# Turning the new keys and values back to token order beside the cached values instead of ahead of the cached keys

## The chip, the core and the metric

The kernel runs on one core of one Trainium2 chip. The metric is the device time of one execution in microseconds. Matrix work is on TensorE (PE), whose weight loads are shown apart as PEld; the other engines are VectorE (DVE), ScalarE (ACT), GpSimd (POOL) and SyncE (SP). Each engine runs its own instructions in the order in which they are written, and waits on semaphores. DMAs are issued by SP, ACT and POOL, and the queues of these engines are written SPq, ACTq and POOLq in the profile.

## What is computed

One inference step through two layers, for a prompt of 256 tokens and a sample group of 8 sequences with 4 new tokens each (288 columns in all). Layer 0 is a gated short convolution beside block-sparse attention; layer 1 is a Mamba-2 mixer; a SwiGLU feed-forward stands behind each. The change lies in layer 0:

```python
q, k, v = heads(q), heads(k), heads(v)       # 8 heads of 64, from h @ w_in
y_b = attend(q, k, v)
# prompt: causal attention over its own 256 tokens
# sample: the 3 best of 8 cached blocks of 256 keys, and its own new tokens
k_prompt, v_prompt = to_pages(kp), to_pages(vp)                          # outputs
k_sample, v_sample = ks.transpose(0, 2, 1, 3), vs.transpose(0, 2, 1, 3)  # outputs
```

The new keys and values are outputs of the kernel in token order. The values are also an operand of the attention. The new keys in token order are an output and nothing else; the scores read the keys as they come out of the projection.

## The kernel before

The input projection of layer 0 leaves everything with channels on the partitions and tokens on the columns, in `BIG`. Behind it stand four stages that matter here.

1. **The own rows** (PE lines 831 to 837). The 4 x 128 channels of the keys, and then of the values, are turned to token order in three tiles each: tokens 0 to 127, tokens 128 to 255, and the 32 sample tokens. That is six turns of four transposes. The results go to `KOUT` and `VTOK`, each `[128, 3, 512]`. The PSUM banks `trb[0]` and `trb[1]` are used in turn. Every turn has a number. An even number lies in `trb[0]` and is copied out by ACT (`tr_act` counts), an odd one lies in `trb[1]` and is copied out by DVE (`tr_dve` counts). `tr_open(n)` makes PE wait until the last turn in the same bank has been copied. Before the first copy ACT waits for `zeroed`, which GpSimd raises behind four memsets (lines 648 to 651); they can't start before the projection has ended, since the buffers lie over its operands. When all six are copied, GpSimd issues 20 stores of the new keys and values.

2. **The cached keys** (PE lines 957 to 971, a loop over 32 slots). A slot is 4 pages of one sequence: 16 pages, so 4 slots, for each of 8 sequences, 1 MiB per slot. PE turns the keys of a slot (line 852) and multiplies the previous slot with the queries (line 873). Two buffers hold a sequence each: `kv`, shown as Z, for the even ones and `kv2`, shown as ring, for the odd ones. The first two sequences are loaded during the projection. The keys of sequence b+2 are loaded slot by slot when PE has turned that slot of sequence b. The first turn waits until every own row is copied (line 850).

3. **The cached values** (PE lines 1013 to 1041, a loop over 8 sequences b). PE turns the probabilities of sequence b+1 (`turn_sample`, line 920), makes a step of the prompt's attention (`prompt_step`, lines 927 to 946), multiplies the values of sequence b (line 985, 32 products in `values(b)`; a last product at line 992 adds the own tokens), and turns the output of sequence b-1 (line 1001). The values use the same two buffers: the loads of sequence b+2 wait for `v_used`, slot by slot, which `values(b)` raises. SP issues 12 of the 16 loads of a sequence (line 547) and ACT issues 4 (line 1389).

   In each round b ACT does in this order: the copy of the turned probabilities (line 1447), the exponentials of the prompt step (lines 1429 and 1431), in round 1 also the exponentials of the sample scores (lines 1397 and 1403), its four loads, and the copy of the output of this round (line 1455). DVE does the masks, maxima and divisions of the prompt step, in round 1 `exp_bias` (line 1859) and the shifts of the sample scores (line 1870), and the convolution.

4. **The output projection and everything behind it.** It starts when the output of the last sequence is turned. Its weights are loaded by SP behind the last values, into the buffer that the values leave.

The order on each engine is written out by hand; there is no planner.

Of the kernel before, what the change touches and what calls it, by code (L numbers as in the profile page):

```python
# [23 lines left out]
P = 128  # L24
# [3 lines left out]
def hybrid_decoder_kernel(  # L28
# [10 lines left out]
    _, NP, D = x_prompt.shape  # L39
    NB, T, _ = x_sample.shape  # L40
    NS = NB * T
    NT = NP + NS
    KD = D // P
    NPOOL, H, PAGE, DH = cache_k.shape
# [7 lines left out]
    MQ, MK, MV = 3 * CA, 3 * CA + H * DH // P, 3 * CA + 2 * H * DH // P  # L52
# [51 lines left out]
    with ExitStack() as ctx:  # L104
# [65 lines left out]
        BIG = Area(Z).take(CC, NT)  # L170
# [7 lines left out]
        KOUT = a.take(3, H * DH)  # L178
        VTOK = a.take(3, H * DH)
# [59 lines left out]
        ident = sb("ident", [P, P])  # L239
# [45 lines left out]
        trb = [ctx.enter_context(nc.psum_tensor(f"trb{i}", [P, 512], F32)) for i in range(2)]  # L285
# [11 lines left out]
        zeroed = sem("zeroed")  # L297
# [8 lines left out]
        tr_full = sem("tr_full")  # L306
        tr_act = sem("tr_act")
        tr_dve = sem("tr_dve")
# [129 lines left out]
        TR_PAR = TR_X + KD  # L438
        TR_HIST = TR_PAR + 2
        TR_KV = TR_HIST + 4  # L440
        TR_K = TR_KV + 6
        N_K = NB * NBLK * 2

        tr_order = [("sample", 0), ("sample", 1)]
        for b in range(1, H + 1):
            tr_order += ([("sample", b + 1)] if b + 1 < NB else []) + [("prompt", b - 1)]
        TR_P = {key: TR_K + N_K + i for i, key in enumerate(tr_order)}
        TR_COA = TR_K + N_K + len(tr_order)
        TR_CO = TR_COA + 2
# [127 lines left out]
        def _(pool):  # L577
            n = [0]
# [66 lines left out]
            pool.memset(KNZ[:, :, :], 0.0)  # L645
            pool.memset(ext[:, :, 0:3], 0.0).then_inc(zeroed, 1)
            pool.wait_ge(acc_full, M_IN0)
            pool.memset(VTOK[:, :, :], 0.0)
            pool.memset(OWN_E_ROWS, 0.0)
            pool.memset(POWN[:, :], 0.0)  # L650
            pool.memset(CUP[:, :, 0:2], 0.0).then_inc(zeroed, 1)
# [6 lines left out]
                if s is stored:  # L658
                    stores[0] += 1

            pool.wait_ge(tr_act, TR_K // 2)
            pool.wait_ge(tr_dve, TR_K // 2)
            for buf, prompt, sample in ((KOUT, k_prompt, k_sample), (VTOK, v_prompt, v_sample)):
                for t in range(NP // PAGE):
                    store(prompt[0, t].rearrange("h q d -> q h d"),
# [44 lines left out]
        def _(pe):  # L710
# [12 lines left out]
            def tr_open(n):  # L723
                if n >= 2:
                    pe.wait_ge(tr_act if n % 2 == 0 else tr_dve, n // 2)
                return trb[n % 2]
# [101 lines left out]
            pe.wait_ge(consts, 3)  # L828
            project(N_IN0, M_IN0, KD, HX0, hx_ready(0), after=after_first)

            for i, m in enumerate((MK, MV)):
                for t in range(3):
                    rows = P if t < 2 else NS
                    bank = tr_open(TR_KV + 3 * i + t)
                    for c in range(H * DH // P):
                        last = pe.transpose(bank[0:rows, c * P:(c + 1) * P], BIG[:, m + c, t * P:t * P + rows], ident[:, :])
                    last.then_inc(tr_full, 1)

            def turn_keys(p):
                b, s = p // KVS, p % KVS  # L840
# [59 lines left out]
            def return_max(part):  # L900
                pe.wait_ge(d_step, part * D_STEPS + 3)
                bank, full = chain_open(part)
                pe.transpose(bank[:, 0:NH], RMT[0:NH, 2, :], ident[0:NH, 0:NH]).then_inc(full, 1)
# [113 lines left out]
            for b in range(NB):  # L1017
                if 1 <= b < NB - 1:
                    turn_sample(b + 1)
                if b and b < NB - 1:  # L1020
                    prompt_step(b)
                if b == NB - 2:
                    prompt_step(b + 1)
                if b == NB - 1:
                    prompt_step(b + 1)
                    prompt_step(b + 2)
                    turn_values(b - 1)
                    turn_history()
                values(b)
                if b == 0:  # L1030
                    turn_max(1)
                    prompt_step(0)
                if b == 1:
                    return_max(1)
                if b == 2:
                    denominators(1)
                if b == 3:
                    turn_own(1)
                if 0 < b < NB - 1:
                    turn_values(b - 1)  # L1040
# [252 lines left out]
        def _(act):  # L1293
# [40 lines left out]
            def copy_transposed(n, dst, src):  # L1334

                act.wait_ge(tr_full, n + 1)
                act.activation(dst, src, ACT.Copy).then_inc(tr_act, 1)
# [37 lines left out]
                    copy_transposed(TR_HIST + 2, hists[:, CC // 3:2 * CC // 3, :], trb[0][:, 0:n].rearrange("p (c j) -> p c j", j=3 * NB))  # L1375


            for i, (dst, t) in enumerate(((KOUT, 0), (KOUT, 1), (KOUT, 2), (VTOK, 0), (VTOK, 1), (VTOK, 2))):
                if i % 2 == 0:
                    rows = P if t < 2 else NS  # L1380
                    if i == 0:
                        act.wait_ge(zeroed, 2)
                    copy_transposed(TR_KV + i, dst[0:rows, t, :], trb[0][0:rows, :])

            def load(cache, b, s, mine):
                page = page_numbers(nc.scalar.engine, b, J4 * s + mine[0], len(mine))
# [63 lines left out]
            def copy_output(b):  # L1450
                act.wait_ge(o_full, b + 1)
                if b >= 2:
                    act.wait_ge(acc_full, marks["o", b - 2])
                act.wait_ge(d_step, b // NH * D_STEPS + 6)
                act.activation(OSB[:, b % 2, :], scb[b % 2][:, :], ACT.Copy, scale=rden[:, b:b + 1]).then_inc(o_copied, 1)
# [4 lines left out]
            for b in range(NB):  # L1460
                if 1 <= b < NB - 1:
                    copy_sample(b + 1)
                if b and b < NB - 1:
                    prompt_step(b)
                if b == NB - 2:
                    prompt_step(b + 1)
                if b == NB - 1:
                    prompt_step(b + 1)
                    prompt_step(b + 2)
                    act.wait_ge(mix_made, 1)  # L1470
                    for k in range(CA):
                        act.activation(HX1[:, k, 0, :], MIX[:, k, :], ACT.Copy).then_inc(hx_hi, 1)
                if b == 1:
                    own_exp(1)
                    for later in range(NH, NB):
                        sample_exp(later)

                for s in range(1, KVS, 2):
                    if b + 2 < NB:
                        act.wait_ge(v_used, b * KVS + s + 1)  # L1480
                        load_values(b + 2, s)
                copy_output(b)
            copy_transposed(TR_COA, coT_a[0:2 + 2 * NB, 0:2 * P], trb[0][0:2 + 2 * NB, 0:2 * P])
            split(N_OUT0)
            def post_norm(i, first_acc, kparts):
# [175 lines left out]
        def _(dve):  # L1661
# [21 lines left out]
            def copy_transposed(n, dst, src):  # L1683

                dve.wait_ge(tr_full, n + 1)
                dve.tensor_copy(dst, src).then_inc(tr_dve, 1)
# [9 lines left out]
            def rest(hx, k, col, src=None):  # L1696

                n_hx[0] += 1
                dve.wait_ge(hx_hi, n_hx[0])
                if col is None:  # L1700
                    ins = dve.tensor_tensor(hx[:, k, 1, :], src, hx[:, k, 0, :], ALU.subtract)
                else:
                    ins = dve.scalar_tensor_tensor(hx[:, k, 1, :], X[:, k, :], par[:, 0, col:col + 1], hx[:, k, 0, :],  # L1703
                                                   ALU.mult, ALU.subtract)
                ins.then_inc(hx_made, 1)
# [40 lines left out]
                last = dve.tensor_copy(KNZ[rows, :, :].rearrange("p (c r) n -> p c r n", r=2)[:, :, r, :],  # L1746
                                       BIG[rows, MK:MK + H // 2, NP:NT])
            link(last)
            for i, (dst, t) in enumerate(((KOUT, 0), (KOUT, 1), (KOUT, 2), (VTOK, 0), (VTOK, 1), (VTOK, 2))):
                if i % 2 == 1:  # L1750
                    rows = P if t < 2 else NS
                    copy_transposed(TR_KV + i, dst[0:rows, t, :], trb[1][0:rows, :])

            def move_scores(b):
                e = b % 2
# [39 lines left out]
            n = NBLK  # L1795
# [210 lines left out]
            for b in range(NB):  # L2006
                if 1 <= b < NB - 1:
                    copy_sample(b + 1)
                if b and b < NB - 1:
                    prompt_step(b)  # L2010
                if b == NB - 2:
                    prompt_step(b + 1)
                if b == NB - 1:
                    prompt_step(b + 1)
                    prompt_step(b + 2)
                    sample_output(b - 1)
                    copy_transposed(TR_COA + 1, coT_a[0:2 + 2 * NB, 2 * P:4 * P], trb[1][0:2 + 2 * NB, 0:2 * P])
                    for k in range(CA):
                        rest(HX1, k, None, MIX[:, k, :])
                if b == 1:  # L2020
                    exp_bias(1)
                    for later in range(NH, NB):
                        shift_scores(later)
                if b == 2:
                    sum_exponentials(1)
                    invert(1)
                if b == 3:
                    own_probabilities(1)
                if 0 < b < NB - 1:
                    sample_output(b - 1)  # L2030
                if b == 1:
                    conv_a_product()
                if 2 <= b <= 4:
                    conv_a_tap(b - 2)
                if b == 5:
                    conv_a_gate()
# [363 lines left out]
```

## Time and profile before

| | us |
|---|---|
| median of 3 runs | 1168.38 (1167.48 to 1168.97) |
| profiled execution, its own time | 1164.51 |
| its span in the trace | 1162.8 |
| PE busy | 1071.0 (92%) |
| PEld busy | 974.5 (84%) |
| DVE busy | 722.9 (62%) |
| ACT busy | 480.4 (41%) |
| POOL busy | 48.1 (4%) |

A busy PE is one in whose pipeline a matmul stands; it is not a PE at its peak. The profiled execution lies 3.9 us below the median of the runs, and 1.7 us of its time lie outside the span. Times of rows are counted from the start of the span.

### The profile page before, as it was taken

The page shows a single profiled execution, that of the slowest core. Times are in us where ns is not written, and L with a number is a line of the kernel's source. Part 1 is how long each engine was busy: PE and PEld are TensorE (multiplying, and loading weights), DVE is VectorE, ACT ScalarE, POOL GpSimd, SP SyncE. Part 2 cuts the span into 40 slices and gives each one's busy share as a digit, 9 for nine tenths or more (in the row PEclk, how much of TensorE's full clock was granted, in tenths as well). Part 3 has the DMA queues.
Part 4 walks back from the last instruction along what each step waited for, and adds up shares of the span by engine and source line. Part 5 has one row for each costly group of instructions (what it writes and reads, how often), then busy time and mean ns, then how long its engine had stood idle before and what let it go on. Part 6 is the DMA issues. An engine that isn't in the chain of part 4 may idle for free.

```text
span 1162.8 us, 21734 instructions
## 1 busy us (share of the span) xinstructions
PE 1071.0 (92%) x8763; PEld 974.5 (84%) x8763; DVE 722.9 (62%) x1391; ACT 480.4 (41%) x814; POOL 48.1 (4%) x93
## 2 busy tenths in 40 slices
PE   5999999887879999999798899889979799999996
PEld 4898888443769999999687899768869699999995
DVE  3454678554566656543589998678864556566344
ACT  4332435232434434432455443454663354434331
POOL 4000400000000000000000001021000000000000
PEclk9899999888989999999899899599989899999997
DMA  9374999999933554545333454089024434544501
GB/s 294 99 257 136 317 349 346 347 348 348 311 109 120 171 168 158 163 160 160 98 109 110 138 171 128 1 271 330 19 82 146 134 108 156 181 151 158 173 28 41
DMA packets 194101, 206.16 MB, mean 177 GB/s; under 512 B 8232, under 2 KB 186621, under 8 KB 193951
## 3 DMA queue, kind: packets, MB, share of 16 engines
q1 hardware_dynamic: 173714, 178.54, 48.5%
q10 hardware_dynamic: 16816, 15.25, 4.2%
q0 software_dynamic: 3472, 10.99, 3.0%
q8 instruction: 69, 1.13, 0.4%
q14 instruction: 30, 0.25, 0.1%
HBM read 192.59 MB, written 12.17 MB: 176 GB/s over the span
## 4 chain that ended last, share of the span: by engine, by line
PE 80%; DVE 11%; DMA 2%; ACT 2%; issue 1%; ACTq 1%; SPq 1%; POOL 1%; DVEq 0%; POOLq 0%
PE acc L762 19%; PE acc L764 19%; PE acc L763 19%; PE scb L738 3%; PE trb L852 3%; DVE WHL L1712 3%; PE scb L873 3%; PE acc L852 2%; PE scb L985 2%; DVE Z L2121 1%; DMA ring<-in_cache_v_dram 1%; DVE Y L2065 1%; DMA ring<-in_state_ssm_dram 1%; PE trb L1114 1%; PE acc L1127 1%
## 5 line engine op out<-in xcount | busy, mean ns | idle before, releaser
L1327 ACT ACTIVATE WHL<-ring 128x1024 fp32r<-128x1024 f32 x224 | 221.5, 1037 | 352.0 <-PE acc L764 352.0
L1712 DVE TENSOR_TENSOR WHL<-ring,WHL 128x1024 fp32r<-128x1024 f32 x224 | 259.9, 1203 | 115.7 <-ACT WHL L1327 115.7
L762 PE MATMUL acc<-HX,WHL 128*128 128x288 f32 x928 | 281.7, 304 | 30.0 <-DVE HX L1703 19.0
L763 PE MATMUL acc<-HX,WHL 128*128 128x288 f32 x928 | 277.8, 299 | 0.0
L764 PE MATMUL acc<-HX,WHL 128*128 128x288 f32 x928 | 277.2, 299 | 0.0
L762 PEld LDWEIGHTS acc<-HX,WHL 128*128 128x128 f32 x928 | 178.8, 193 | 33.4 <-issue 29.0
L763 PEld LDWEIGHTS acc<-HX,WHL 128*128 128x128 f32 x928 | 180.2, 194 | 0.3
L764 PEld LDWEIGHTS acc<-HX,WHL 128*128 128x128 f32 x928 | 179.7, 194 | 0.0
L762 PE MATMUL acc<-G,WHL 128*128 128x288 f32 x480 | 145.3, 303 | 12.6 <-DVE G L1703 7.7
L763 PE MATMUL acc<-G,WHL 128*128 128x288 f32 x480 | 143.6, 299 | 0.0
L764 PE MATMUL acc<-G,WHL 128*128 128x288 f32 x480 | 143.2, 298 | 0.0
L762 PE MATMUL acc<-HID,WHL 128*128 128x288 f32 x352 | 104.8, 298 | 0.0
L762 PEld LDWEIGHTS acc<-G,WHL 128*128 128x128 f32 x480 | 92.3, 192 | 14.2 <-issue 9.3
L763 PE MATMUL acc<-HID,WHL 128*128 128x288 f32 x352 | 103.5, 294 | 0.0
L764 PE MATMUL acc<-HID,WHL 128*128 128x288 f32 x352 | 103.4, 294 | 0.0
L763 PEld LDWEIGHTS acc<-G,WHL 128*128 128x128 f32 x480 | 92.9, 194 | 0.2
L764 PEld LDWEIGHTS acc<-G,WHL 128*128 128x128 f32 x480 | 92.8, 193 | 0.0
L763 PEld LDWEIGHTS acc<-HID,WHL 128*128 128x128 f32 x352 | 66.5, 189 | 0.2
L764 PEld LDWEIGHTS acc<-HID,WHL 128*128 128x128 f32 x352 | 66.4, 189 | 0.0
L762 PEld LDWEIGHTS acc<-HID,WHL 128*128 128x128 f32 x352 | 66.0, 187 | 0.2
L2086 DVE TENSOR_TENSOR Z<-acc,RR 128x288 f32<-128x288 f32 x44 | 20.0, 455 | 50.0 <-PE acc L764 50.0
L2290 DVE SCALAR_TENSOR_TENSOR ring<-ring,dec,acc 128x128 f32<-128x128 f32 x128 | 34.7, 342 | 13.4 <-PE acc L1127 12.5
(377 smaller groups left out, 1460.9 us busy)
## 6 DMA issues: line engine op xcount, KB each, us to landing
ring<-in_l_w_in_dram SPq DMA_DIRECT2D x32, 1024.0 KB, 5.4
ring<-in_l_ffn_gate_dram SPq DMA_DIRECT2D x22, 1024.0 KB, 5.3
ring<-in_l_ffn_up_dram SPq DMA_DIRECT2D x22, 1024.0 KB, 5.3
ring<-in_l_ffn_down_dram SPq DMA_DIRECT2D x16, 1024.0 KB, 5.2
Z<-in_cache_k_dram SPq DMA_DIRECT2D x52, 256.0 KB, 7.0
ring<-in_cache_k_dram SPq DMA_DIRECT2D x52, 256.0 KB, 7.0
Z<-in_cache_v_dram SPq DMA_DIRECT2D x48, 256.0 KB, 7.8
ring<-in_cache_v_dram SPq DMA_DIRECT2D x48, 256.0 KB, 7.0
```

The source lines that it names most:

```text
L738: pe.matmul(stat[:, 0:NT], ones[:, :], SQ[:, n_sq[0] % 4, :], start=(count == 0), stop=(count == total - 1)).then_inc(sq_used, 1)
L762: pe.matmul(out, w[:, 0, at:at + P], rhs[:, k, 0, :], start=(k == 0), stop=False)
L763: pe.matmul(out, w[:, 0, at:at + P], rhs[:, k, 1, :], start=False, stop=False)
L764: last = pe.matmul(out, w[:, 1, at:at + P], rhs[:, k, 0, :], start=False, stop=(k == kdim - 1))
L852: last = pe.transpose(TURNED[q][jp][:, hh * P:(hh + 1) * P], keys[:, s, 4 * q + hh, 2 * jp:2 * jp + 2, :].rearrange("p j d -> p (j d)"), i ...
L873: last = pe.matmul(scb[e][g * QT:(g + 1) * QT, s * P:(s + 1) * P], QZ[:, e, q, hh * QT:(hh + 1) * QT], KTB[p % 2][:, jp, q, hh * P:(hh + 1 ...
L985: last = pe.matmul(bank[j * QT:(j + 1) * QT, :], S[:, b, s, j * QT:(j + 1) * QT], held[:, s, :, j, :], start=(s == 0), stop=(s == KVS - 1 ...
L1114: last = pe.transpose(trb[n % 2][:, hh * P:(hh + 1) * P], st[:, (q * PG + hh) * NST:(q * PG + hh + 1) * NST], ident[:, :])
L1327: act.activation(WHL[part_of[i]][:, i % 2, 0, half], ring[:, slot_of(u), half], ACT.Copy).then_inc(w_hi, 1)
L1712: dve.tensor_tensor(w[:, i % 2, 1, half], ring[:, slot_of(unit_of[i]), half], w[:, i % 2, 0, half], ALU.subtract).then_inc(w_lo, 1)
L2086: free(dve.tensor_tensor(us[:, r, :], take()[:, 0:NT], RR[:, :], ALU.mult))
L2290: last = dve.scalar_tensor_tensor(st[:, k, :], st[:, k, :], dec[:, k, b:b + 1], bank[:, hh * NST:(hh + 1) * NST], ALU.mult, ALU.add)
```

## The change

Ahead of the cached keys only the sample tokens' tiles are turned: one turn for the keys (copied by ACT) and one for the values (copied by DVE, which now waits for `zeroed` too). The four turns of the prompt's tokens get numbers in the order of the turns in the loop over the cached values. In round 0, behind `values(0)` and the first prompt step, PE turns both value tiles; in round 1, behind `values(1)` and `return_max(1)`, both key tiles. ACT copies the first tile of each pair at the end of its round, behind its loads and the copy of the output. DVE copies the second behind its prompt step; in round 1 that is ahead of `exp_bias`. GpSimd clears 512 columns of `VTOK` instead of 1536, and its stores wait for the turns of round 1.

```diff
-        TR_K = TR_KV + 6
+        TR_K = TR_KV + 2
+        TURN_LATER = (((VTOK, MV, 0), (VTOK, MV, 1)), ((KOUT, MK, 0), (KOUT, MK, 1)))
+        tr_order = [("sample", 0), ("sample", 1), ("later", 0), ("later", 1)]
         for b in range(1, H + 1):
             tr_order += ([("sample", b + 1)] if b + 1 < NB else []) + [("prompt", b - 1)]
+            if b == 1:
+                tr_order += [("later", 2), ("later", 3)]
# GpSimd
-            pool.memset(VTOK[:, :, :], 0.0)
+            pool.memset(VTOK[:, 2, :], 0.0)
-            pool.wait_ge(tr_act, TR_K // 2)
-            pool.wait_ge(tr_dve, TR_K // 2)
+            pool.wait_ge(tr_act, TR_P["later", 2] // 2 + 1)
+            pool.wait_ge(tr_dve, TR_P["later", 3] // 2 + 1)
# TensorE
+            def turn_own_rows(n, m, t):
+                rows = P if t < 2 else NS
+                bank = tr_open(n)
+                for c in range(H * DH // P):
+                    last = pe.transpose(bank[0:rows, c * P:(c + 1) * P], BIG[:, m + c, t * P:t * P + rows], ident[:, :])
+                last.then_inc(tr_full, 1)
             for i, m in enumerate((MK, MV)):
-                for t in range(3):
...
+                turn_own_rows(TR_KV + i, m, 2)
...
                 if b == 1:
                     return_max(1)
+                if b < 2:
+                    for i, (_, m, t) in enumerate(TURN_LATER[b]):
+                        turn_own_rows(TR_P["later", 2 * b + i], m, t)
# ScalarE
+            act.wait_ge(zeroed, 2)
+            copy_transposed(TR_KV, KOUT[0:NS, 2, :], trb[0][0:NS, :])
...
                 copy_output(b)
+                if b < 2:
+                    dst, _, t = TURN_LATER[b][0]
+                    copy_transposed(TR_P["later", 2 * b], dst[:, t, :], trb[0][:, :])
# VectorE
+            dve.wait_ge(zeroed, 2)
+            copy_transposed(TR_KV + 1, VTOK[0:NS, 2, :], trb[1][0:NS, :])
...
+                if b < 2:
+                    dst, _, t = TURN_LATER[b][1]
+                    copy_transposed(TR_P["later", 2 * b + 1], dst[:, t, :], trb[1][:, :])
                 if b == 1:
                     exp_bias(1)
```

## Rows read from the trace of the kernel before

**Rows 1.** The chain of waits, 95 to 300 us: start, duration, what.
```profile
109.64 1.38 POOL Z L648
...
114.83 1.15 PE trb L852 x8
...
260.45 10.70 DMA ring<-in_cache_v_dram
271.19 3.64 PE scb L985 x16
```

**Rows 2.** The timeline, 104 to 122 us: start, duration, engine, line, operation.
```profile
110.19 1.32 DVE L1746 COPY Z<-Z 64x128 f32<-64x128 f32 x2
...
111.02 0.36 POOL L650 MEMSET Z<- 128x256 f32 x1
...
111.46 0.60 ACT L1337 ACTIVATE Z<-trb 128x512 f32<-128x512 f32 x1 [12.46 <-POOL Z L651]
...
114.09 0.60 ACT L1337 ACTIVATE Z<-trb 128x512 f32<-128x512 f32 x1 [0.75 <-PE trb L836]
114.59 0.68 DVE L1686 COPY Z<-trb 32x512 f32<-32x512 f32 x1 [0.70 <-PE trb L836]
```

**Rows 3.** Windows: length, busy time of each engine, granted clock, DMA share, GB/s.
```profile
110.00:117.00 7.00, 4.83 (x40) 3.82 (x38) 5.04 (x14) 2.87 (x5) 2.50 (x6) 1.00 0.00 0
117.00:243.00 126.00, 118.08 (x1820) 92.05 (x1820) 87.98 (x222) 49.52 (x103) 12.10 (x19) 0.97 1.09 342
...
222.00:228.00 6.00, 5.06 (x23) 1.50 (x27) 2.58 (x10) 2.20 (x9) 0.00 (x0) 0.51 1.07 341
...
230.00:232.00 2.00, 2.00 (x23) 1.10 (x21) 0.95 (x5) 0.22 (x1) 0.00 (x0) 1.00 1.10 349
```

**Rows 4.** The timeline of PE, 205 to 305 us; in brackets idle time and releaser.
```profile
219.31 0.66 PE L920 MATMUL trb<-ident,Z 128*128 128x128 f32 x4
...
222.94 0.90 PE L934 MATMUL trb<-ident,SQ 128*128 128x128 f32 x3 [2.12 <-DVE SQ L1925]
223.77 6.17 PE L985 MATMUL scb<-ring,Z 128*32 128x512 f32 x32
229.77 1.02 PE L992 MATMUL scb<-Z 128*32 128x512 f32 x2
230.72 0.22 PE L903 MATMUL acc<-ident,RMT 4*128 4x4 f32 x1
...
231.44 0.66 PE L920 MATMUL trb<-ident,Z 128*128 128x128 f32 x4
...
234.15 3.64 PE L985 MATMUL scb<-Z 128*32 128x512 f32 x32
...
243.89 1.12 PE L920 MATMUL trb<-ident,Z 128*128 128x128 f32 x4
...
247.34 0.69 PE L944 MATMUL acc<-Z 128*64 128x128 f32 x2
...
248.82 3.90 PE L985 MATMUL scb<-ring,Z 128*32 128x512 f32 x32
```

**Rows 5.** The timeline of ACT, 205 to 310 us.
```profile
225.31 0.69 ACT L1455 ACTIVATE Y<-scb,small 128x512 f32<-128x512 f32 x1 [3.21 <-issue]
225.90 0.65 ACT L1447 ACTIVATE Z<-trb 128x256 f32<-128x256 f32 x2
...
231.18 0.22 ACT L1397 ACTIVATE Z<-Z 64x16 f32<-64x16 f32 x1 [3.76 <-DVE Z L1859]
...
234.93 3.46 ACTq L1389 DMA_DIRECT2D ring<-in_cache_v_dram  x4
238.49 0.69 ACT L1455 ACTIVATE Y<-scb,small 128x512 f32<-128x512 f32 x1 [3.48 <-PE scb L985]
```

**Rows 6.** The timeline of SP, 60 to 330 us.
```profile
226.89 10.21 SPq L547 DMA_DIRECT2D ring<-in_cache_v_dram  x12
238.28 12.57 SPq L547 DMA_DIRECT2D Z<-in_cache_v_dram  x12
```

## What I expect

> **What bounds the kernel now.** I read the chain of waits first. Up to 109.3 us it is the input projection. Then it leaves PE: the memset of `VTOK` at 109.64, the other memsets, and copies and turns of own rows until the first turn of cached keys at 114.83 [rows 1]. The timeline shows why. ACT waited 12.46 us, the last part of it for GpSimd, and starts at 111.46; the last copies begin at 114.09 on ACT and at 114.59 on DVE [rows 2]. Next come the windows. From 110 to 117 us the DMA engines move nothing; from 117 to 243 they move 342 GB/s without a break [rows 3]. So the stage of cached keys and values is bound by the transfers, and its clock starts when the first slot of keys is turned. Last I look at what closes the stage: PE waits at 271.19 for values of sequence 5 [rows 1]. A gain ahead of the stage arrives at its end only if the stream of transfers is not interrupted on the way. The three engines that serve `values(b)` decide that, because a buffer is loaded again only when `values(b)` has read it.
>
> **Part 1: the shorter lead-in, -3.05 us.** Four of six turns go, and two thirds of one memset. Memsets of 256 and 1536 columns took 0.36 and 1.38 us [rows 1, 2], 0.80 ns per column between them; 512 columns are then 0.57 us, and `zeroed` comes 0.81 us earlier, at 110.6. ACT's one copy (0.60) ends at 111.25. DVE first finishes its two copies of line 1746 at 110.19 + 1.32 = 111.51, then copies the sample values (0.68): 112.22. Before, that copy ended at 114.59 + 0.68 = 115.27 [rows 2]. The second group of key turns needs it, so all of the key stage moves by 115.27 - 112.22 = 3.05 us. DVE's 111.51 is now late next, so the memset itself is worth nothing more; its 0.81 us is hidden.
>
> **Part 2: what is moved.** Four turns of about 0.5 us on PE (a whole `turn_sample` is a 0.66 us row that overlaps its neighbours by 0.1), two copies of 0.60 on ACT, two of 0.69 on DVE, and 20 stores on GpSimd. The stores move 1.2 MB, some 3.4 us of the stream; they leave its start and come back near 244 us. As work that is small. As order it isn't.
>
> *Round 0.* `later 0` lies in `trb[0]`, and so does the next `turn_sample(2)`. Before, PE ran that at 219.31 [rows 4], waiting for a copy long done. Now `tr_open` waits for ACT's copy of `later 0`, and ACT has the prompt's exponentials, four loads and the copy of the output ahead of it. In the trace of before, the instruction behind the copy of the output starts at 225.90 [rows 5]. Shifted by 3.05 this is 222.85, the copy takes 0.60, and PE resumes at 223.5. It would have got there at 216.3 without the two turns, 217.2 with them, so it stands still 6.3 us. Queued behind the waiting turn are the prompt step and `values(1)`.
>
> PE's clock is the second price. After an idle time of 2.12 us PE resumed at 222.94, and the granted clock was 0.51 from 222 to 228 (the 1.2 GHz level) and 1.00 again from 230; the 32 products of `values(1)` took 6.17 us there and 3.64 at the full clock [rows 3, 4]. I take 6 us of half clock behind each long idle. From `turn_sample` to `values` the same work in round 3 ran at the low clock from 243.89 to 248.82, 4.93 us; without the prompt's values, which round 1 doesn't have, it is 3.45 (243.89 to 247.34) [rows 4]. So `values(1)` starts at 223.5 + 3.45 = 226.95. Its first 2.5 us are at the low clock (11 products), the other 21 at 0.114 us each: 4.9 us, and 0.85 for line 992. It ends at 232.7; before it was 230.7 [rows 4]. The gain is gone, and PE is 2.0 us late.
>
> *Round 1.* DVE's copy of `later 3` stands ahead of `exp_bias`. PE has two turns to do for it (0.95) and the copy takes 0.69: with the handover, 1.8 us more for `exp_bias` and for ACT's line 1397 behind it. That was at 231.18 [rows 5]; now it is 231.18 + 2.0 + 1.8 = 235.0. From there ACT needs 238.49 - 231.18 = 7.3 us to the copy of the output, in which the four loads are 3.46 [rows 5], then 0.59 and 0.60 for the copy of `later 2`: 243.5. `turn_sample(3)`, before at 231.44, waits for this. PE resumes at the low clock, needs 4.93 us, and `values(2)` starts at 248.4 instead of 234.15 [rows 4]: 14.3 us late.
>
> Of the Trainium skill two rules bear here. "DMA: Bandwidth & Descriptors", section on issuing engines, says that all issued transfers run on the same 16 engines, and that issuing from several engines saves only sequencer time, which is usually small beside the transfer. The row of the four loads says 3.46 us of ACT's time [rows 5]. If that were negligible, PE would resume about 3 us sooner in each round.
>
> **Part 3: what arrives at the end, +8 us in sum.** SP issued the loads of sequence 4 from 238.28 [rows 6]. They joined a queue: 40 slots of 1 MiB and 1.2 MB of stores are 43.1 MB, and at 342 GB/s from 117 they are through at 243 [rows 3], so sequence 4's bytes began to flow at 243. Now the first loads wait for `v_used` of `values(2)`, 8 products at the low clock, 1.8 us: 250.2. The bytes of sequence 3 are through by about 244, so the engines are idle apart from the stores. With 1 to 2 us from issue to the first bytes (the first second behind the issue at 117.02 was half empty), sequence 4 begins to flow at 251.2 to 252.2, 8.2 to 9.2 us later than before. From there the stream is saturated: a sequence is 12 us of transfers, and `values(3)` (PE resumes at 248.4, so it reaches it at about 257) frees its buffer before the 12 us are over. PE's wait for sequence 5 at 271.19 moves with the stream, and so does all behind it, including the weights of the output projection. PE's own chain by the same count is 8.4 us late. I take +8, a little under both, since ACT's loads may be quicker with emptier queues. Copies on DVE, the wait for `zeroed` there and the stores cost nothing more: `exp_bias` carries the first, 111.51 is behind 110.6 for the second, and the third run in the hole.
>
> Sum on the profiled execution: span 1162.8 + 8.0 = 1170.8, its own time 1164.51 + 8.0 = 1172.5. The median lies 3.9 above: 1168.4 + 8.0 = **1176.4**.
>
> Bounds. The lead-in has little doubt (-2.8 to -3.2). If PE has its full clock after both waits, 4.93 becomes 2.71 (231.44 to 234.15 [rows 4]), 3.45 in proportion 1.9, and `values(1)` takes 3.64; then `values(2)` starts at 243.4, its first slot is read at 244.3, and the bytes flow from about 246: +3. If the clock stays low for twice as long and the queue restarts slowly, it is +11. The prices between are all of rows at one of the two clocks; I stand by the low one, which each idle time over 2 us showed.
>
> **Rivals.** *A: the transfers carry the gain to the end, 1165.3.* The stream starts 3.05 us earlier and stays full, since each moved piece is under 1 us on engines at 41 to 62%. "Perfetto Trace Analysis" of the Trainium skill, optimization strategy, recommends interleaving regimes with different contended engines, which is this change. For it: 342 GB/s without a break, and PE has idle time beside the values. Against it: ACT's order. It decides if ACT copies within 2 us of the turn, and the rows have 6 and 10 us.
>
> *B: the hole is filled, within 0.2%.* PE is late in rounds 1 and 2, but the queues hold more work than I count, so that the bytes of sequence 4 flow 3 us later than before instead of 8; the slack of PE against the transfers takes the rest. For it: `values(2)` began 4.1 us before the loads of sequence 4 did. Against it: a 14 us delay is longer than the 12 us of one buffer. It gives 1168 to 1170.
>
> *C: twice the price, 1181 to 1184.* The hole also drops PE's clock in rounds 4 to 7, as PE waits for each slot, and every chain from there to the output projection runs at half speed. For it: the wait at 271.19 was followed by 3.64 us for 16 products. Against it: this happens before as well, and by then both are late by the same.
>
> **How the numbers follow.** My case holds 0.72, A 0.09, B 0.09, C 0.10. A range of 1169.5 to 1181 leaves out A, most of B and half of C. A change under 0.2% (2.3 us) can't be told from none: faster 0.09, same 0.08, slower 0.83.
>
> **What would show it.** Right: the first line-852 turn near 111.3; PE idle of 5 to 7 us ahead of `turn_sample(2)` and 8 to 10 ahead of `turn_sample(3)`, both released by ACT's copy of a turn; a window near 245 to 250 us with well under 348 GB/s; `values(2)` at about 248. Step 1 is wrong if the key stage starts later than 112; step 2 if PE isn't released by that ACT copy; step 3 if there is no hole in the transfers, and then A or B holds.

## The result, and the profile after

The changed kernel took 1178.14 us (median of 7 runs, 1173.63 to 1184.11) against 1169.25 us before (7 runs), a ratio of 1.0075 with a 95% interval of 1.0050 to 1.0101. A second set on another occasion gave 1181.21 us and 1.0100 (1.0074 to 1.0126). It is slower by 9 to 12 us; 1176.4 was predicted, in a range of 1169.5 to 1181.

The profiled execution of the changed kernel was the slowest of the seven, 1184.11 us with a span of 1182.4, so spans must not be subtracted as they are. I count from the last product of the first projection, which starts at 109.29 before and at 111.46 after, to the first product of the output projection (301.08 and 312.20). This stretch, called the stage below, is 191.8 us before and 200.7 after: **+8.9 us**, where +8 was predicted. 2.2 us of the difference of the spans lie ahead of it and 8.5 behind it.

First the lead-in, from the timelines of the changed kernel at 106 to 118 us and of GpSimd. Columns: start, duration, engine, line, operation, idle time and releaser.

```profile
111.82 0.53 POOL L652 MEMSET Z<- 128x512 f32 x1 [92.98 <-PE acc L768]
...
112.36 0.64 DVE L1754 COPY Z<-Z 64x128 f32<-64x128 f32 x2
...
112.72 0.59 ACT L1346 ACTIVATE Z<-trb 32x512 f32<-32x512 f32 x1 [11.55 <-POOL Z L655]
113.04 0.68 DVE L1694 COPY Z<-trb 32x512 f32<-32x512 f32 x1
113.45 1.07 PE L858 MATMUL trb<-ident,Z 128*128 128x128 f32 x8 [0.82 <-ACT Z L1346]
```

DVE's last copy of own rows ends at 113.72, 2.26 us behind the start of the last product; before it was 115.27, 5.98 behind it [rows 2]. That is 3.7 us less. PE gains a little less: line 850 lets the first group of key turns go when ACT has copied its own rows, and only the second group waits for DVE's. The first group (line 858, 852 before) starts 1.99 us behind the last product, and before 5.54 [rows 1]. So the lead-in is 3.5 us shorter for PE, and the values of sequence 0 begin 3.5 us earlier too. DVE's two copies of `KNZ` took 0.64 us here and 1.32 before [rows 2].

Then PE's timeline at 205 to 320 us, to be held against [rows 4]:

```profile
225.30 1.09 PE L926 MATMUL trb<-ident,Z 128*128 128x128 f32 x4 [6.26 <-ACT Z L1346]
...
228.72 5.02 PE L991 MATMUL scb<-ring,Z 128*32 128x512 f32 x32
233.57 1.02 PE L998 MATMUL scb<-Z 128*32 128x512 f32 x2
...
245.21 1.09 PE L926 MATMUL trb<-ident,Z 128*128 128x128 f32 x4 [8.87 <-ACT Z L1346]
...
250.10 4.58 PE L991 MATMUL scb<-Z 128*32 128x512 f32 x32
...
283.89 1.06 PE L991 MATMUL scb<-ring,Z 128*32 128x512 f32 x8 [2.85 <-DMA ring<-in_cache_v_dram]
```

Line 926 is `turn_sample` (920 before). PE stood still for 6.26 and for 8.87 us, and both times a copy by ACT of a moved turn (line 1346) released it. ACT's timeline shows what that copy waited behind, as against [rows 5]: the loads (2.69 and 3.43), the copy of the output, in round 1 the exponentials as well.

```profile
221.19 2.69 ACTq L1394 DMA_DIRECT2D Z<-in_cache_v_dram  x3
223.98 0.69 ACT L1460 ACTIVATE Y<-scb,small 128x512 f32<-128x512 f32 x1 [3.25 <-issue]
224.56 0.59 ACT L1346 ACTIVATE Z<-trb 128x512 f32<-128x512 f32 x1
...
236.60 0.21 ACT L1402 ACTIVATE Z<-Z 64x16 f32<-64x16 f32 x1 [6.04 <-DVE Z L1865]
...
240.36 3.43 ACTq L1394 DMA_DIRECT2D ring<-in_cache_v_dram  x4
243.89 0.69 ACT L1460 ACTIVATE Y<-scb,small 128x512 f32<-128x512 f32 x1 [3.45 <-issue]
244.47 0.59 ACT L1346 ACTIVATE Z<-trb 128x512 f32<-128x512 f32 x1
```

The windows of the changed kernel, in the columns of [rows 3], show two holes in the transfers, and SP's timeline why. The loads of sequence 3 go out from 230.89, 119.4 us behind the last product where it was 117.6 before [rows 6]; the stream had run ahead till then, and from 230 to 232 nothing moves. The loads of sequence 4, issued from 238.28 before [rows 6], now go out from 252.24.

```profile
230.00:233.00 3.00, 3.00 (x24) 0.76 (x20) 1.18 (x4) 0.56 (x3) 0.00 (x0) 0.74 0.19 62
230.00:240.00 10.00, 6.34 (x55) 2.51 (x47) 5.30 (x18) 3.08 (x11) 0.00 (x0) 0.84 0.66 213
240.00:245.00 5.00, 0.00 (x0) 0.00 (x0) 1.20 (x3) 1.55 (x4) 0.00 (x0) 0.50 0.96 321
245.00:250.00 5.00, 4.79 (x17) 3.28 (x17) 1.44 (x4) 1.18 (x6) 4.62 (x7) 0.50 0.79 205
250.00:255.00 5.00, 5.00 (x35) 1.29 (x34) 1.74 (x7) 0.53 (x3) 5.00 (x8) 0.80 0.44 71
255.00:260.00 5.00, 5.00 (x49) 3.07 (x51) 3.44 (x14) 1.35 (x4) 3.59 (x7) 1.00 1.00 332
```

```profile
230.89 9.61 SPq L551 DMA_DIRECT2D ring<-in_cache_v_dram  x12
252.24 9.53 SPq L551 DMA_DIRECT2D Z<-in_cache_v_dram  x12
```

### The profile page after: what moved, and what is told of

Its sections match the earlier page's. It is cut to its first block, busy times and chain, and to the rows that moved or that the text cites. A ratio compares the mean times of both kernels' runs of the same rounds, so it can differ in the third digit from the quotient of the medians.

```text
span 1182.4 us, 21734 instructions
## 1 busy us (share of the span) xinstructions
PE 1078.4 (91%) x8763; PEld 982.7 (83%) x8763; DVE 721.9 (61%) x1391; ACT 479.9 (41%) x814; POOL 47.3 (4%) x93
## 4 chain that ended last, share of the span: by engine, by line
PE 61%; DVE 9%; SPq 4%; DMA 2%; ACT 2%; issue 1%; POOL 0%; ACTq 0%; DVEq 0%; POOLq 0%
PE acc L766 17%; PE acc L768 17%; PE acc L767 16%; SPq L551 3%; PE scb L742 3%; DVE WHL L1720 2%; DVE Z L2130 1%; DMA ring<-in_state_ssm_dram 1%; DVE Y L2074 1%; PE trb L1123 1%; DMA ring<-in_l_w_out_dram 1%; PE acc L1270 1%; PE acc L1136 1%; PE acc L1069 1%; DVE RR L1699 1%
## 5 line engine op out<-in xcount | busy, mean ns | idle before, releaser
L2299 DVE SCALAR_TENSOR_TENSOR ring<-ring,dec,acc 128x128 f32<-128x128 f32 x128 | 34.7, 341 | 15.8 <-PE acc L1136 15.1
```

What stands on the lines that cost most here:

```text
L2299: last = dve.scalar_tensor_tensor(st[:, k, :], st[:, k, :], dec[:, k, b:b + 1], bank[:, hh * NST:(hh + 1) * NST], ALU.mult, ALU.add)
```

## The experiments

Twelve runs, eleven of an edited kernel and one of the changed kernel again, each timed beside the kernel before on the same chip. A ratio rests on 6 to 12 executions, a stage on the one trace of the run, so a difference of 1 or 2 us in the stage alone shows little. One of the twelve executions of act_early took 2063.93 us; the others lie between 1165.4 and 1174.2. The theory is the prediction's: `turn_sample` is blocked by ACT's copy of a moved turn, PE's delay reaches the loads, and the loads set the end.

| run | stage, us | ratio to before (95%) |
|---|---|---|
| before | 191.8 | |
| after_again | 200.7 | 1.0100 (1.0074 to 1.0126) |
| wait_only | 200.5 | 1.0081 (1.0061 to 1.0102) |
| act_early | 190.5 | 0.9988 (0.9969 to 1.0008) |
| no_later | 192.8 | 1.0018 (0.9997 to 1.0038) |
| memset_only | 190.1 | 0.9994 (0.9968 to 1.0019) |
| round0_early | 196.9 | 1.0044 (1.0023 to 1.0065) |
| round1_early | 196.8 | 1.0038 (1.0015 to 1.0061) |
| sp_issue | 193.8 | 1.0009 (0.9987 to 1.0031) |
| best | 193.2 | 0.9972 (0.9947 to 0.9997) |
| best_sp | 192.5 | 0.9993 (0.9969 to 1.0016) |
| all_later | 190.3 | 0.9984 (0.9959 to 1.0009) |
| all_later_sp | 192.7 | 0.9990 (0.9964 to 1.0017) |

**after_again**: no edit.

> The changed kernel once more, as the base of the comparison. Its one profile so far had a span of 1182.4 us, of which the stretch from the end of the first projection to the output projection was 8.9 us longer than before, 2.2 us lay ahead of it and 8.5 us behind it. Theory (PE blocked behind ACT's copies): the stretch is again 8 to 9 us longer, since it is an order of instructions, and what lies ahead of and behind it varies from run to run; the median is 8 to 9 us above before. Rival (the change also costs behind the stage, by another alignment of the weights): the rest behind 312 us is again 8 us longer and the median is 16 us above.

The stage is 200.7 us again, in a second trace, as the theory has it. The rest behind it, 1180.2 - 310.24 = 870.0 us, was again some 8 us longer than before's 861.7, as the rival said of the trace; but the median is 11.5 above before and not 16, and the rest is taken up below.

**wait_only**: the order alone, in the kernel before.

```diff
                 if 1 <= b < NB - 1:
+                    if b <= 2:
+                        pe.wait_ge(o_copied, b)
                     turn_sample(b + 1)
```

> The kernel before with nothing moved; PE only waits in rounds 1 and 2 until ACT has copied the output of the round before (o_copied) ahead of turn_sample. This is the order that the change brings in, without its turns and without the shorter lead-in. Theory: PE idles 6 us and 7 to 9 us, the transfers have a hole at sequence 4, and the kernel is 8 to 10 us slower than before (11 if nothing catches up; the copy itself and DVE's copy ahead of exp_bias are missing, which were some 3 us). Rival (PE's idle time beside a stream of transfers is hidden): within 1 us of before.

It measured 1.0081, 9.5 us slower. The waits of its PE at 105 to 310 us (waiter, releaser, sum, times, longest) and the hole in its windows are much like those of the changed kernel:

```profile
PE trb L920 <- ACT Y L1457: 14.4, 2, 7.7
```

```profile
245.00:250.00 5.00, 5.00 (x21) 3.01 (x23) 1.53 (x5) 1.64 (x6) 0.00 (x0) 0.50 0.61 209
250.00:255.00 5.00, 5.00 (x52) 1.69 (x44) 1.82 (x8) 0.00 (x0) 0.00 (x0) 0.98 0.44 133
```

No turn was moved and no store, and the stage is 8.7 us longer all the same: the wait alone makes a loss of this size. The rival, by which PE's idle time beside the stream is hidden, falls. The sum isn't quite the same, though. This kernel has no shorter lead-in to set against the loss, and lacks the two copies that stand in the chain of the changed one (some 3 us by the text above). That the two cancel is argued and not shown.

**act_early**: ACT's copies ahead of its exponentials and loads.

```diff
+                if b in (0, 1):
+                    dst, _, t = TURN_LATER[b][0]
+                    copy_transposed(TR_P["later", 2 * b], dst[:, t, :], trb[0][:, :])
                 if b == 1:
                     own_exp(1)
...
                 copy_output(b)
-                if b < 2:
...
```

> ACT's copies of the first later turn move ahead of its exponentials and loads in both rounds, nothing else. Theory (it is the place of these copies that costs): both idle times of PE (6.3 and 8.9 us) vanish, the transfers run without a hole and the lead-in's 3 us arrive: 3 to 4 us under before, 11 to 12 under the changed kernel. Rival (the work of the four turns, or the stores of 1.2 MB in the middle of a saturated stream, costs as well): same as before, within 1 us, since the stores take 3.4 us of the stream wherever they stand and only the lead-in's shift could pay, eaten by the turns.

The loss is gone, 0.9988. The gain of 3 to 4 us isn't seen either: the median lies 1.3 us under before and the stage is 1.3 us shorter. The interval reaches from 3.6 us under before to 0.9 above, so it holds no change and, at its edge, 3 us as well; the rival is the nearer one, but the time doesn't exclude the theory. The values of sequence 0 begin 3.6 us earlier than before, counted from the projection. Then the trace differs from before in two places. The windows of the run:

```profile
200.00:210.00 10.00, 8.31 (x155) 7.11 (x154) 5.97 (x13) 3.03 (x6) 0.00 (x0) 1.00 1.10 348
210.00:220.00 10.00, 7.41 (x52) 3.49 (x53) 7.08 (x27) 1.46 (x5) 0.00 (x0) 0.96 0.85 273
220.00:230.00 10.00, 10.00 (x55) 3.95 (x53) 2.83 (x9) 2.57 (x8) 0.00 (x0) 0.70 0.99 322
230.00:240.00 10.00, 7.74 (x68) 3.56 (x67) 6.76 (x20) 3.54 (x11) 8.56 (x13) 1.00 1.05 334
```

and the waits of its SP and PE:

```profile
SPq L551 <- PE acc L858: 13.9, 15, 7.9
SPq L551 <- PE scb L991: 6.8, 3, 3.5
```

```profile
PE acc L914 <- DVE Z L1883: 5.9, 1, 5.9
```

From 210 to 240 us the stream moves 310 GB/s in the mean, against 346 before in the same windows: 30 x 36 / 348 = 3.1 us of transfers not done. Before, SP waited for PE once on its way through the loads, at their start (11.8 us); here it waited 18 times. SP issues the values of sequence 0 at 184.29, 74.6 us behind the last product, against 83.6 before: the stream is 9.0 us earlier, since it starts earlier and has no stores at its head, and PE only 3.6. So it catches up with PE and is held by it, most at the change from keys to values. That the gain is lost there is the reading that fits these numbers; no run takes it apart.

**no_later**: the shorter lead-in alone.

```diff
-                if b < 2:
-                    for i, (_, m, t) in enumerate(TURN_LATER[b]):
-                        turn_own_rows(TR_P["later", 2 * b + i], m, t)
...
-            pool.memset(VTOK[:, 2, :], 0.0)
+            pool.memset(VTOK[:, :, :], 0.0)
...
+            step(pool.memset(KOUT[:, 0:2, :], 0.0))
```

> The changed kernel without the four turns of the prompt's keys and values and their copies: those rows are cleared by GpSimd instead, so the prompt's values and the two prompt outputs are left out. Shows what the shorter lead-in is worth by itself. Theory: 3.0 us under before, as the whole stage moves by 3.05 us. Rival (the transfers or PE take the gain back before the stage ends): within 1 us of before.

No gain, 1.0018. It doesn't measure what it was meant to, because of its own clearing. Its timeline:

```profile
110.94 2.38 DVE L1747 COPY Z<-Z 64x128 f32<-64x128 f32 x2
...
112.06 0.95 POOL L663 MEMSET Z<- 128x1024 f32 x1
...
112.89 0.63 PE L857 MATMUL trb<-ident,Z 128*128 128x128 f32 x4 [1.68 <-ACT Z L1342]
```

The same two copies took 2.38 us beside the longer clearing, DVE's copy of the sample rows came at 113.36, PE waited 1.7 us and had its clock at 0.50 in the window from 114 to 117. Its values of sequence 0 began only 0.4 us earlier than before. The lead-in's worth by itself stays open.

**memset_only**: the shorter memset alone, in the kernel before.

```diff
-            pool.memset(VTOK[:, :, :], 0.0)
+            pool.memset(VTOK[:, 2, :], 0.0)
```

> The kernel before with one edit: GpSimd clears 512 columns of the values' buffer instead of 1536. The prediction held this worth nothing, since DVE's two copies (line 1746, 1.32 us there) would end at 111.51 in any case. In the changed kernel these two copies took 0.64 us, with a shorter memset beside them, and in the kernel without later turns 2.38 us, with more clearing beside them. Theory (DVE's copies are slowed by GpSimd's memsets): the copies take 0.6 to 0.8 us here, the first own row is copied about 0.8 us earlier, and the stage of the keys starts 0.8 us earlier; the median moves under 1 us, within the noise. Rival (the 1.32 us belongs to the copies): they take 1.32 us again.

The copies took 0.64 us, and the copy behind them began at 113.08, 1.57 us behind the last product (2.25 before):

```profile
112.41 0.64 DVE L1746 COPY Z<-Z 64x128 f32<-64x128 f32 x2
113.08 0.69 DVE L1686 COPY Z<-trb 128x512 f32<-128x512 f32 x1
```

The theory holds on the copies: 0.64, 1.32 and 2.38 us for the same two instructions, in the order of how long GpSimd cleared beside them. The key stage starts 0.9 us earlier (4.63 us behind the last product, 5.54 before) where 0.8 was expected. The time didn't move beyond the noise. The stage of this one trace is 1.7 us shorter than before, more than that of act_early with its much shorter lead-in.

**round0_early** and **round1_early**: the edit of act_early for one round each (`if b in (0,)` and `if b in (1,)`).

> The changed kernel with ACT's copy moved ahead of its loads in round 0 alone; round 1 keeps its order. Theory (two blocks in a row, and only what stands last before the loads of sequence 4 counts): the idle time of PE in round 0 falls from 6.3 to 2.3 us, the one in round 1 stays 9 us, and all behind it is 4 to 5 us earlier than in the changed kernel: 4 to 6 us above before. Rival (the first block alone makes the loss, since it stops the stream first): back at the kernel before, within 1 us.

> The changed kernel with ACT's copy moved ahead of its exponentials and loads in round 1 alone. Theory: the idle time of 6.3 us in round 0 stays, the one of 8.9 us in round 1 goes; PE reaches the values of sequence 2 some 10 us earlier than in the changed kernel, and the time is 0 to 3 us above before. Rival (each block is worth its idle time, 6.3 and 8.9): 6 us above before minus the lead-in of 3.7, so the same 2 to 3 us; the two differ in the trace only, by where the transfers have their hole. If it comes out as far above before as the changed kernel, both fall.

Each block undone gives back about half: the loss of 10.2 us (the mean of the two ratios of the changed kernel, 1.0087) becomes 5.1 and 4.4. The stage falls by 3.8 and 3.9 us, and by 10.2 with both. The expectation that only the last block counts is right for round 0 (4 to 6 us above before) and missed for round 1: 0 to 3 us above before was expected, 4.4 was measured. Its interval (1.8 to 7.1 us) overlaps with that, but the stage is 5.0 us longer too. With the copy of round 1 ahead, PE waits 5.7 us for DVE (line 914) a little later, behind the exponentials of round 2, which on ACT stand behind the same loads and copy.

**sp_issue**: SP issues the loads of sequences 2 and 3 in full, ACT none.

```diff
-                        if (b < 2 or g != ACT_K) if cache is cache_k else (s, g) not in ACT_PAGES:
+                        if (b < 2 or g != ACT_K) if cache is cache_k else (b in (2, 3) or (s, g) not in ACT_PAGES):
...
-                    if b + 2 < NB:
+                    if b >= 2 and b + 2 < NB:
```

> The changed kernel with the four loads of rounds 0 and 1 issued by SP instead of ACT. ACT's copies stay behind the copy of the output, but 3.3 to 3.5 us of issuing no longer stand ahead of them. Theory: PE's idle times fall from 6.3 to about 3 and from 8.9 to about 5.5 us; the kernel is 4 to 6 us faster than the changed one, still 3 to 5 above before. Rival (issuing is small beside the transfer, and SP gets slower by the same work, 16 loads of 0.79 us instead of 12 for a sequence, which is more than the 12.05 us that the transfers need): no gain, since SP's queue is now the later one.

The order of the copies is as in the changed kernel, and yet the loss is gone but for 1.1 us that can't be told from none (1.0009), where 3 to 5 us above before was expected. PE's waits of the run at 200 to 260 us:

```profile
PE trb L926 <- ACT Z L1346: 8.2, 2, 5.3
```

15.1 us of waiting became 8.2, 3.5 less in each round, and the stage 6.9 us shorter, 1 to 3 more than expected, though still 2.0 above before. The Trainium skill, "DMA: Bandwidth & Descriptors", section "Issuing engines are not separate DMA queues", calls the time for issuing usually small beside the transfer. Here it isn't: an issue of 256 KB took ACT 0.6 to 0.9 us, and at 348 GB/s the 256 KB themselves take 0.75. It is small only beside the 7 us from issue to landing. And it stands on an engine for which PE waits: moving eight issues took 6.9 us off the stage.

**best**, **best_sp**, **all_later**, **all_later_sp**. best is act_early with DVE's copy of `later 3` behind `exp_bias`; the suffix sp adds the edit of sp_issue; all_later also moves the sample tokens' turns to just ahead of round 0:

```diff
+                if b == 1:
+                    exp_bias(1)
                 if b < 2:
                     dst, _, t = TURN_LATER[b][1]
                     copy_transposed(TR_P["later", 2 * b + 1], dst[:, t, :], trb[1][:, :])
                 if b == 1:
-                    exp_bias(1)
...
+            for i, m in enumerate((MK, MV)):
+                turn_own_rows(TR_P["own", i], m, 2)
             turn_sample(0)
```

> The changed kernel with ACT's copies ahead of its loads in both rounds (as the run act_early) and DVE's copy in round 1 behind exp_bias instead of ahead of it. act_early had its stage 1.3 us shorter than before although its first values were multiplied 3.6 us earlier: PE then idled 5.9 us for DVE in round 2, behind ACT's exponentials, loads and copy of the output. Theory (PE's and ACT's chain of rounds 0 to 2 binds, not the transfers): 0.7 us less of that chain, so 0 to 1 us under act_early and 2 us under before. Rival (the transfers bind there): no difference from act_early.

> As the run best, and the eight loads of rounds 0 and 1 issued by SP instead of ACT (as the run sp_issue, which took 3.3 us off each of PE's two idle times and brought the changed kernel back to the kernel before). Theory: the chain of rounds 0 to 2 through ACT loses another 3.5 us per round, the idle time of 5.9 us in round 2 falls to about 2, and the kernel is 3 to 5 us under before. Rival (with the copies ahead of the loads already, ACT's issuing is hidden): as best.

> As the run best, and the two turns of the sample tokens are moved too, to just ahead of round 0, so that nothing stands between the projection and the first turn of cached keys but the release of the last bank. Theory: the key stage starts 1.8 to 2 us earlier than in best (the first turn 0.5 instead of 2.0 us behind the projection), and since the chain of PE binds and not the transfers, about 1 us of it is left after the two turns and copies are done in the idle time ahead of round 0 (PE waits 2.0 us for DVE there): 1 to 2 us under best. Rival: the wait of 2.0 us for DVE ahead of round 0 grows by DVE's copy (0.7 us), and nothing is left.

> Both together: all own rows turned beside the values, ACT's copies ahead, DVE's copy behind exp_bias, and SP issuing the loads of rounds 0 and 1. Theory: the gains add to best's, 4 to 7 us under before. Rival (the transfers bind as soon as PE's chain is short): as best_sp, 3 to 5 us under before, since 56 slots of 1 MiB at 348 GB/s are 169 us in any order.

best is the one kernel whose interval lies under before, 0.9972, just. That isn't enough to call it faster: it is one interval of a dozen, and the stage of its trace is 1.4 us longer than before, so nothing in the trace accounts for a gain. The other three can't be told from before or from best. best_sp did shorten PE's wait for DVE in round 2 from 5.2 to 1.8 us, as expected, and nothing of the expected 3 to 5 us is seen: PE then waited for transfers instead, 7.5 us in four places against 3.9 in two. The first key turn of all_later came 1.0 us behind the last product instead of 2.0, and nothing of it was left at the values of sequence 0, as its rival said: they begin 101.0 us behind the last product, in best 100.9. For all_later_sp theory and rival both missed, since 3 us or more under before was expected of either and 1.2 was measured. Without the block in rounds 0 and 1 the orders of act_early and of these four end the stage at 190 to 193 us. That the transfers and PE's chain take turns in binding there fits the waits; that it is all there is wasn't shown.

## Why the prediction was right, point by point

Times here are counted from the last product of the projection (prediction minus 109.3, trace minus 111.5).

- *The lead-in, -3.05 us.* The end was right, the size 0.7 short at DVE's copy (3.7) and 0.5 at PE's first key turn (3.5). The step that failed is that DVE's two copies would take 1.32 us in any case, so that the memset is worth nothing. They took 0.64, because less clearing ran beside them.
- *Round 0.* PE waits 6.3 us for ACT's copy: 6.26. It resumes at 114.2: 113.8. It ran at the low clock behind that: 3.42 us to `values(1)` and 5.02 for it, where 3.45 and 4.9 were worked out.
- *Round 1.* 8 to 10 us: 8.87. Resumed at 134.2: 133.8. `values(2)` at 139.1: 138.6. All three terms (PE late from round 0, `exp_bias` behind DVE's copy, ACT's 7.3 us) came out; from ACT's line 1402 at 236.60 to its copy of the output at 243.89 it was 7.3. By `values(3)` PE is 8.1 us late, 8.4 in the text, since the wait of 3.85 us that PE had in round 2 before (line 908, at 242.48) is gone. The text says there that PE resumes at 248.4; that is where `values(2)` starts, and PE resumes at 243.5.
- *The hole.* Loads of sequence 4 issued at 140.9: 140.8. The bytes of sequence 3 through at 134.7: 135.0 (246.5 in the trace). From 247 to 254 only stores move, 0.70 MB of their 1.18, at 24 GB/s and less from 250 to 253; sequence 4 flows in earnest from 254, near the late end of 1 to 2 us behind the issue. The other 0.48 MB of stores, issued until 258.6, run beside its first loads; at 348 GB/s that is 1.4 us of the stream. The text had them all in the hole, at no cost. PE's wait for sequence 5, at 161.9 before, ended at 172.4: 10.5 us later, 1 to 2 more than the +8.2 to +9.2 of the text, which is about this share of the stores. Not in the text is the first hole, from 230 to 232, behind the block of round 0; the hole itself doesn't add to the end, since sequence 3 is through in time and sequence 4 waits for `values(2)`; the block does, as it makes PE late for round 1 (round0_early).
- *The end of the stage.* +8 predicted, +8.9 measured. Some 1.6 of the 10.5 us are caught up again between sequence 5 and the output projection; where wasn't tried apart. That the sum is only 0.9 off is in part luck, as the stores and what was caught up about cancel.
- *What was wrong in the reading.* The text has the stage bound by the transfers, and a gain ahead of it arriving if the stream isn't interrupted on the way. Rival A rested on that. With the block removed the stream starts earlier and is interrupted all the same, 3.1 us in sum and most of it at the change from keys to values (act_early). So the kernel before seems to have two limits within some 3 us of each other, and 342 GB/s without a break showed only one. A did not happen in the changed kernel. Its 1165.3 wasn't seen in act_early either, where ACT copies early, as A asks; the interval there doesn't exclude 3 us, though. B, the filled hole, did not happen. C did not happen in the stage: from 255 to 300 us the granted clock was 0.92, and 0.89 before. The 1181.21 of the second set has C's number without its mechanism.

**Behind the stage.** In both profiled executions of the changed kernel layer 1's mixer took 292 us, against 284.9 in the profiled one of before. The windows of that stretch, for after, before and best:

```profile
604.60:896.50 291.90, 265.13 (x1983) 241.61 (x1982) 230.64 (x516) 141.50 (x264) 18.63 (x19) 0.89 0.44 137
```

```profile
592.00:876.90 284.90, 259.22 (x1983) 235.84 (x1982) 230.70 (x516) 141.62 (x264) 18.63 (x19) 0.91 0.45 141
```

```profile
598.10:890.10 292.00, 265.31 (x1983) 241.76 (x1982) 230.77 (x516) 141.39 (x264) 18.60 (x19) 0.89 0.44 138
```

The instructions are the same and the granted clock is 0.89 instead of 0.91. best is as long, and has the lowest ratio of all kernels here. Between the same two instructions of DVE the fourteen traces have 283.9 (round1_early) to 292.5 us, with wait_only at 287.4 and act_early at 289.0. So this isn't a price of the change's order by itself, and it is why one trace against another gave 19.6 us where the medians differ by 9 to 12. Whether the changed kernel is at the long end more often, which would explain why its median lies up to 2.6 us beyond the stage's 8.9, stays open: two profiles don't settle it.

## What to carry to other kernels

When a step is moved to a place where its engine is idle, look at who reuses its buffer next and at everything that stands ahead of its copy on the copying engine; the copy was 0.6 us, and PE waited 6 to 9 for it. A DMA issue is work of the engine that issues it: moving eight of them away took 6.9 us off the stage, reordering the copies 10.2. And before a gain at the head of a saturated stream is booked, look for the point where the stream waits for its consumer once it is no longer late.

## What the runs showed of the hardware

DVE's pair of copies of `[64, 128]` from SBUF to SBUF took 0.64 us in the changed kernel, 1.32 in the one before and 2.38 in the one without later turns, and 0.64 in the kernel before with only the memset shortened. Taken one by one, a copy with no memset beside it took 0.22 us. Each copy that met memsets ended 0.07 or 0.08 us behind the end of one: the first in no_later took 2.14 us and ended at 113.08, and the last of five memsets in a row ended at 113.01. In the changed kernel the memset of 512 columns was over when the copies began, and the first met only the shorter ones behind it (0.41 us). The Trainium skill, "SBUF — State Buffer", on the ports, says that DVE and GpSimd share one pair of ports, that a DVE copy can enter a mode that takes it, and that the second one to issue then stands still until the first is done. The traces agree on the copies; in no_later the copy wasn't let in between the memsets either.

PE's granted clock was at 0.50 (1.2 GHz) from 225 to 230 and from 245 to 250 us, behind the idle times of 6.26 and 8.87 us, and from 114 to 117 in the kernel without later turns, behind 1.68. Behind the 2.05 us of idle time that end at 212.17 in the changed kernel it stayed at 1.00:

```profile
212.00:216.00 4.00, 3.83 (x35) 1.40 (x36) 3.60 (x13) 0.00 (x0) 0.00 (x0) 1.00 0.91 297
```

So the length of an idle time alone doesn't tell whether the clock falls. The prediction took the fall for sure on the ground of idle times over 2 us. Here it came, but what decides it was not tried.
